# Down-projection of a gated feed-forward layer: five chunks of two tile pairs behind a plain pair, against four chunks of 2, 3, 3 and 3 pairs with no plain pair between

## The reference, cut to what matters

```python
h = _modulated_norm(x, norm_ffn_g[l], shift2, scale2)
hid = _causal_dwconv(h @ w_up[l], ffn_conv_w[l], ffn_conv_b[l])    # 3 taps, 2 x 3072 columns
act, val = jnp.split(hid, 2, axis=-1)
x = x + gate2[:, None, :] * ((jax.nn.gelu(act) * val) @ w_down[l])  # 3072 x 1024
```

## Time and profile before

| | us |
|---|---|
| median of 3 runs (lowest, highest) | 1511.46 (1511.32, 1512.23) |
| the profiled execution | 1512.01 |
| its span | 1510.3 |
| TensorE busy | 1494.3 (99%) |
| VectorE busy | 1251.8 (83%) |
| ScalarE busy | 819.4 (54%) |
| GpSimd busy | 406.9 (27%) |
| a store of a spilled block (512 KB), issue to landing, median | 2.8 to 3.0 |

### The profile page before, as it was taken

One profiled execution on the slowest core, in us unless ns is written; L12 is line 12 of the kernel. 1 busy time (PEld: TensorE's weight loads), 2 busy tenths in 40 slices (PEclk: granted clock), 3 DMA queues, 4 the chain that ended last, 5 costly groups with the idle time before them and its releaser, 6 DMA issues.

```text
span 1510.3 us, 19809 instructions
## 1 busy us (share of the span) xinstructions
PE 1494.3 (99%) x6790; PEld 1232.6 (82%) x6790; DVE 1251.8 (83%) x1584; ACT 819.4 (54%) x1237; POOL 406.9 (27%) x313
## 2 busy tenths in 40 slices
PE   7999999999999999999999999999999999999998
PEld 4888888888888888888888878888888888888887
DVE  7987888777777786698869999999999987777776
ACT  5368888734454363423436555555555553444447
POOL 0033434522222223000100233333333331333325
PEclk9999999999999999999999999999999999999999
DMA  9431233373443364572521244444444436777722
GB/s 367 174 118 57 60 91 94 121 266 115 159 139 125 109 216 146 187 225 91 172 68 34 63 167 154 155 157 152 152 152 153 154 112 233 251 251 251 251 67 112
DMA packets 212227, 231.12 MB, mean 153 GB/s; under 512 B 9920, under 2 KB 164896, under 8 KB 211360
## 3 DMA queue, kind: packets, MB, share of 16 engines
q1 hardware_dynamic: 212128, 229.86, 45.4%
HBM read 167.95 MB, written 61.87 MB: 152 GB/s over the span
## 4 chain that ended last, share of the span: by engine, by line
PE 93%; DVE 4%; DMA 1%; issue 0%; ACT 0%; SPq 0%; DVEq 0%; ACTq 0%
PE ps L900 75%; PE ps L980 6%; PE ps L1001 2%; PE ps L1285 1%; PE ps L1131 1%; PE ps L1043 1%; PE ps L1266 1%; PE ps L1188 1%; PE ps L1089 1%; DVE wop L1969 1%; DMA xtok<-in_x 1%; DVE hq L2629 1%; DVE hidw L2686 1%; DVE n L2621 0%; PE ps L1078 0%
## 5 line engine op out<-in xcount | busy, mean ns | idle before, releaser
L1361 ACT ACTIVATE wop<-raw 128x512 fp32r<-128x512 f32 (+1 forms) x541 | 307.1, 571 | 348.8 <-PE ps L900 227.8
L1969 DVE TENSOR_TENSOR wop<-raw,wop 128x512 fp32r<-128x512 f32 (+1 forms) x541 | 373.8, 695 | 103.2 <-ACT wop L1361 101.5
L733 POOL TENSOR_TENSOR raw<-raw,raw 128x512 f32<-128x512 f32 (+1 forms) x69 | 101.6, 1472 | 857.9 <-DVE wop L1969 341.6
L900 PE MATMUL ps<-hq,wop 128*128 128x512 f32 x888 | 213.7, 390 | 0.2 <-DVE hq L2629 0.2
L900 PEld LDWEIGHTS ps<-hq,wop 128*128 128x128 f32 x888 | 166.4, 188 | 36.1 <-DVE hq L2629 1.0
L900 PE MATMUL ps<-yq,wop 128*128 128x512 f32 x792 | 191.3, 390 | 0.0
L900 PE MATMUL ps<-dq,wop 128*128 128x512 f32 x840 | 190.6, 389 | 0.0
L900 PEld LDWEIGHTS ps<-dq,wop 128*128 128x128 f32 x840 | 157.7, 188 | 32.7
L900 PEld LDWEIGHTS ps<-yq,wop 128*128 128x128 f32 x792 | 148.0, 188 | 30.7
L1983 DVE TENSOR_TENSOR ps<-ps,snap_p 128x512 f32<-128x512 f32 x136 | 94.5, 695 | 43.1 <-PE ps L900 42.2
L1376 ACT ACTIVATE snap_p<-ps 128x512 f32<-128x512 f32 x136 | 81.2, 597 | 81.9 <-PE ps L900 81.7
(11 more groups left out here) (296 smaller groups left out, 2586.4 us busy)
## 6 DMA issues: line engine op xcount, KB each, us to landing
dq<-hid_keep SPq DMA_DIRECT2D x35, 1024.0 KB, 7.0
raw<-in_w_in SPq DMA_DIRECT2D x96, 256.0 KB, 4.0
raw<-in_w_up SPq DMA_DIRECT2D x96, 256.0 KB, 3.3
hid_keep<-part_b SPq DMA_DIRECT2D x40, 512.0 KB, 3.0
hid_keep<-part_t SPq DMA_DIRECT2D x20, 512.0 KB, 2.8
raw<-in_w_down SPq DMA_DIRECT2D x80, 128.0 KB, 2.3
gate_keep<-tg SPq DMA_DIRECT2D x16, 512.0 KB, 4.1
quarter_ring<-in_w_ada SPq DMA_DIRECT2D x64, 128.0 KB, 2.3
```

The source lines that it names most:

```text
L733: nc.gpsimd.tensor_tensor(s1, a21, a22, ALU.add).then_inc(s_made, 1)
L900: done = nc.tensor.matmul(bank, left[:, w, lk, :], right[:, x, rk, :], start=(first and w == 0 and x == 0), stop=(last and w == 1), skip_g ...
L1361: nc.scalar.activation(wop[n % 4][:, 0, 0:depth[n], :], raw[slot][:, 0:depth[n], :], ACT.Copy).then_inc(f_hi, 1)
L1969: V.tensor_tensor(wop[n % 4][:, 1, 0:kd, :], raw[slot_of[n][0]][:, 0:kd, :], wop[n % 4][:, 0, 0:kd, :].bitcast(F32), ALU.subtract).then_in ...
```

## The change

Eleven pairs are now spilled and go through the seven-product scheme; unit M is gone, and the four D chunks hold 2, 3, 3 and 3 pairs (16 units, D0 to D15). D0 stands right behind U23. The two-pair chunk has seven 8 KB buffers `dq_first`, all in the region that U23 reads, each filled once U23 has done the product named in `D_FIRST_FREED`. The three-pair chunks share nine 12 KB buffers, so from the third block on a block of a chunk waits until the chunk before has read a buffer in its last unit.

```diff
-        DK = 2
-        D_FREED = (1, 1, 2, 3, 3, 4, 4, 5, 5, 6, 6, 7, 7)
+        DK = 3
+        D_FIRST_AT, D_FIRST_FREED = (0, 8, 32, 40, 16, 24, 48), (1, 1, 4, 4, 6, 6, 7)
+        D_AT = [("MH", 8), ("MH", 20), ("MH", 32), ("MH", 44), ("MY", 0), ("MY", 36), ("MY", 12), ("MY", 24), ("MY", 48)]
+        D_FREED_U, D_FREED_D = (3, 3, 5, 7), (2, 4, 5, 6, 7)
...
-        NP = FT // 2 - 2
-        CHUNKS = [(c, c + DK) for c in range(0, NP, DK)]
-        SEQ += [("M", 0)] + [("D", (KT // 2) * c + i) for c in range(len(CHUNKS)) for i in range(KT // 2)] + [("L", 0)]
+        NP = FT // 2 - 1
+        CHUNKS = [(max(c, 0), c + DK) for c in range(NP % DK - DK, NP, DK)]
+        SEQ += [("D", (KT // 2) * c + i) for c in range(len(CHUNKS)) for i in range(KT // 2)] + [("L", 0)]
...
             def block_back(c, i):
+                n = 7 * (c - 1) + i
+                if c == 0:
+                    sp.wait_ge(*used_at[first_op["U", FT - 1] + D_FIRST_FREED[i] - 1])
+                elif n < len(D_FREED_U):
+                    sp.wait_ge(*used_at[first_op["U", FT - 1] + D_FREED_U[n] - 1])
...
                 elif n < len(dq):
+                    sp.wait_ge(*used_at[first_op["D", KT // 2 - 1] + D_FREED_D[n - len(D_FREED_U)] - 1])
                 else:
+                    c_before, i_before = divmod(n - len(dq), 7)
+                    sp.wait_ge(*used_at[first_op["D", KT // 2 * (c_before + 2) - 1] + i_before])
...
+                next_chunk = u // (KT // 2) + 1 if kind == "D" and u // (KT // 2) < len(CHUNKS) - 1 else None
+                ahead = 4 if next_chunk == 1 else 2
                 weights(pos, 0, 2)
+                if next_chunk is not None and u % (KT // 2) == 3:
+                    block_back(next_chunk, ahead)
...
+                if next_chunk is not None and u % (KT // 2) == 3:
+                    block_back(next_chunk, ahead + 1)
                 weights(pos, 3, 4)
+                if spilling and u == FT - 1:
+                    part_to_dram(j, "t2")
+                    block_back(0, 3)
+                    block_back(0, 4)
+                    block_back(0, 5)
+                    part_to_dram(j, "t4")
+                    part_to_dram(j, "b22")
+                    block_back(0, 6)
...
+                if next_chunk is not None and u % (KT // 2) == 3:
+                    for i in range(ahead + 2, 7):
+                        block_back(next_chunk, i)
...
-            def middle_down(m, pos):
...
+                    if (kind, u, w) == ("D", 0, 0):
+                        tap(FT - 1, 1, pos - 1)
+                    if (kind, u, w) == ("D", 0, 6):
+                        gelu(FT - 1)
+                    if (kind, u, w) == ("D", 1, 6):
+                        hid_high(FT - 1)
...
-            def middle_evict(m, pos):
...
+                    if (kind, u) == ("D", 0) and w < 4:
+                        conv_tap(FT - 1, w // 2, w % 2 + 1, pos - 1)
+                    if (kind, u, w) == ("D", 1, 3):
+                        gate_mul(FT - 1)
+                    if (kind, u, w) == ("D", 2, 3):
+                        hid_low(FT - 1)
```

More of the change, by code:

```diff
@@ L337, in plain @@
         def plain(item):
-            return item[0] in "BML" or item in (("G", 0), ("O", 3)) or item[0] == "U" and item[1] < PLAIN
+            return item[0] in "BL" or item in (("G", 0), ("O", 3)) or item[0] == "U" and item[1] < PLAIN
         def row_of(t):
@@ L702, in _ @@
                     part_to_dram(j + 1, "b11")
-                if (kind, u) == ("U", FT - 1):
-                    for i in range(3, 7):
-                        block_back(0, i)
-                if kind == "D" and u // 4 < len(CHUNKS) - 1:
-                    for i in range(2 * (u % 4), min(2 * (u % 4) + 2, 7)):
-                        block_back(u // 4 + 1, i)
+                if next_chunk is not None and u % (KT // 2) == 1:
+                    for i in range(ahead - 2):
+                        block_back(next_chunk, i)
+                if next_chunk is not None and u % (KT // 2) == 2:
+                    for i in range(ahead - 2, ahead):
+                        block_back(next_chunk, i)
+                if next_chunk is not None and u % (KT // 2) == 3:
+                    for i in range(ahead + 2, 7):
+                        block_back(next_chunk, i)
             for i in range(NB):
@@ L921, in unit @@
                 resident = YA_BLOCKS if item[0] == "A" else UP_BLOCKS if item[0] == "U" else NORM_BLOCKS
-                b11_, t1_, t2_, b22_, t3_, b21_, t4_ = resident if chunk is None else (dq[(7 * chunk + i) % len(dq)][:, :, :, :].bitcast(F32R) for i in range(7))
+                b11_, t1_, t2_, b22_, t3_, b21_, t4_ = resident if chunk is None else (dq_of(chunk, i)[:, :, :, :].bitcast(F32R) for i in range(7))
                 def t_ready(i):
@@ L1250, in _ @@
             quarter = [LB[0][:, 0, :], LB[0][:, 1, :], LB[1][:, 0, :], LB[1][:, 1, :]]
-            def middle_down(m, pos):
-                n0 = first_op["M", 0]
-                bank = BANKS[pos % 2][m % 2]
-                if m < 2:
-                    set_free(pos, m)
-                else:
-                    pe.wait_ge(down_used, m - 1)
-                for kk in range(2):
-                    n = n0 + 2 * (m // 4) + kk
-                    ready(n)
-                    pe.wait_ge(hid_lo, kk + 1)
-                    x_of = hid[hid_slot(2 * NP + kk)]
-                    for h in range(2):
-                        for w, x in PRODUCTS:
-                            done = nc.tensor.matmul(bank[:, h, :], wop[n % 4][:, w, m % 4, :], x_of[:, x, H[h]],
-                                                    start=(kk == 0 and w == 0 and x == 0), stop=(kk == 1 and w == 1))
-                done.then_inc(tile_done, 1)
             def last_down(i):
```

80 lines of the change are left out of this document (21 added, 59 removed).

## The result

| | before | changed |
|---|---|---|
| median us (lowest, highest) | 1511.46 (1511.32, 1512.23) | 1531.85 (1527.36, 1533.62) |
| ratio, 95% interval | | 1.0129 (1.0118 to 1.0141) |
| the profiled execution | 1512.01 | 1529.82 |
| its span | 1510.3 | 1527.9 |
| mean granted TensorE clock | 0.999 | 0.996 |

The changed kernel is slower, as forecast, but by 20 us and not by 7. It lies outside the range of 1511.0 to 1522.5. Its executions also spread over 6 us, those of the kernel before over 1 us.

What follows compares the result with a forecast made beforehand. TensorE, 99% busy, was taken as the bound, so time falls with fewer matmuls and rises with new waits. Terms -2.7 + 5.0 + 1.2 + 2.7 + 1.0 = +7.2 us gave 1518.7 against 1511.46; range 1511.0 to 1522.5.

Steps and rivals of the forecast that it cites:

- item 5: Ends of chunks 1 and 2: A11 lands late, join 1 ends 0.5 us late, twice: 1.0 us, from 0 to 3.
- 1, matmuls: Unit M's 96 matmuls go, D units grow from 840 to 924: 12 fewer, 2.7 us saved.
- Item 2: Loads at U23's end: A11 of D1 lands behind the backlog, D0's seventh product starts at +13.2, a 5.0 us stall.
- The lower bound of item 2: Stores free in the queue: DVE's passes decide D0's seventh product, +10.6 after U23's end, a stall of 2.4 us.
- The store's price of 1.25 us: Queue at U23's end: each half-megabyte store was taken to hold the queue for 1.25 us.
- Item 3: D1 and D2: one added DVE pass ahead of join 0 costs 0.6 us per unit, 1.2 in all.
- Item 4: End of chunk 0: A12 lands late, delaying POOL's S4, ACT's copy and snap 0; D4's third product stalls 2.7 us.
- A: Rival: the queue keeps up, only DVE's added passes are left; D0 stalls 2.4 us, total 1511.5; chance 0.12.
- B: Rival: nothing waits, so the kernel is faster, 1508.8 us, decided at D0's seventh product at +8.2; chance 0.10.
- C: Rival: queue slower with 1.5 MB blocks and stores mixed, 2.93 us per MB (358 GB/s), total 1529; chance 0.03.
- The entry of about 5 us: Expected sign: a new TensorE wait in D0 ahead of the t4 product, released by DVE's join behind a weights DMA.
- sign of being wrong: Two given: D0's seventh product starting before +10 after U23's end, or TensorE showing no wait at D4.

Runs made afterwards that it cites:

- t2_early: The changed kernel with the store of part t2 of pair 10 issued ahead of block 2 instead of behind it: 1530.78 us, ratio 1.0129.
- quarter_loads: The changed kernel with t2 stored ahead of block 2 and blocks 2 to 6 of the first chunk cut to a quarter of their bytes: 1522.80 us.
- late_stores: The changed kernel with t2 stored ahead of block 2 and the last two stores (t4, b22 of pair 10) moved behind block 6: 1531.62 us, ratio 1.0132.
- weights_first: The changed kernel with weights A22 and A12 issued ahead of the blocks in a chunk's last unit: 1529.92 us, ratio 1.0123.

## Why the prediction was wrong

The direction was right, and so was the main mechanism, loads behind a backlog once M's 21.8 us of cover are gone. Two steps failed by size: the sum of item 5, which came to 1.0 us and measured 3.9, and the price of a wait, which the forecast put at its own length, with nothing for the clock that falls behind it (5.8 us). By its items:

| item | forecast | idle in the profile | clock behind it |
|---|---|---|---|
| 1, matmuls | -2.7 | -2.7 | |
| 2, D0 | 5.0 | 2.47 + 3.09 | 3.5 |
| 3, D1 and D2 | 1.2 | 0.59 + 0.64 | |
| 4, D4 | 2.7 | 0.98 + 2.38 | 1.7 |
| 5, D8 and D12 | 1.0 | 2.20 + 1.68 | |

- **Item 2** is wrong in how it comes about and nearly right in its sum (5.6 for 5.0), which is luck. A11 landed at +14.3 instead of +11.7, because the sum began with block 2 in an idle queue, and the seventh product started at +15.8 instead of +13.2. It did not cost 2.6 more idleness there because D0 was already held for 2.47 and slowed for 1.8 before it. The chain from t2's store over ACT's buffer, two bias passes and the snap wasn't in the forecast. t2_early shows that it hides in the same delay.
- **The lower bound of item 2** (+10.6) was measured: +9.8 in quarter_loads. The store's price of 1.25 us held: in late_stores the two stores landed 1.3 us each behind what was ahead of them. Item 3 was right to a tenth, 1.23 for 1.2.
- **Item 4** named the right chain for the third product, A12, POOL's S4, copy, snap, and was short by 0.7: A12 landed at +5.7 instead of +4.7. It passed over the second product, held for 0.98 by A22 and S1, which is part of the same delay. weights_first removes both waits.
- **Item 5** is the mis-sized term: 3.9 us for 1.0. A11 came at +12.8 instead of +11.0. Of these 1.8 us, 1.0 lies again in the first load: block 2 (issued at 1360.47) took 7.5 us, not the 6.45 of a queue taken as idle. Most of the rest lies in the two weight tiles among the blocks, which landed 0.8 and 1.0 behind the block ahead, not 0.55. The blocks came 3.6 to 3.9 us apart, as taken. The bound that I gave, 3 us, was below it too.
- **Nothing on the clock.** The forecast priced a wait at its own length. Behind D0's two waits and D4's second one the clock was at half for most of 4 us: 5.8 us in all with the tenths elsewhere, and 1.3 more for the ends of eight stretches. With item 5, 2.9, and items 2 and 4, 1.2, these are 11.2 us, which makes 18.4 of 7.2. In the median there are some 2 us more than in the profiled execution. The mean granted clock was 0.996 in the two shortest executions (1527.36 and 1529.82) and 0.993 or 0.994 in the three longest, so the clock was low for longer there; which waits it followed, no profile shows.
- **The rivals.** A and B fell at D0's seventh product, which started at +15.8 and not at +10.6 or +8.2. C gave 1529, near the time, for a reason that isn't there: the stretch 1265.90 to 1270.10 moved 414 GB/s, as the earlier trace rows had it, and not 358, and the 1.5 MB blocks of D7 landed 3.6 to 3.9 us apart and not 4.4. A time that fits is no proof of its mechanism; D0's idle 5.6 us, against the 7.8 of C, speaks against it too.
- **What would show it.** The entry of about 5 us became two of 2.5 and 3.1; the one at D4 was there, and block 6 took 10.7 us to land, for 11 forecast. That last match is luck: it was issued at +3.2 and not at 0, because its place in the queue is behind the last store, whose part ACT made late, and it landed at +13.9 and not at +11.3. Neither sign of being wrong came up, so they could not have caught the error. The busy time of TensorE in the page was the first sign of the rest: fewer matmuls, more busy time.

## What to carry to other kernels

When a change takes the only work that hides a queue of loads, follow the last small load in the queue and the one buffer that is freed by a store in it, because an engine that works in order puts every join, snap and copy behind them; moving one item ahead moves the wait to the item that is now last. Price a TensorE wait of 2 us and more at its length plus up to 3 us of half clock, as these runs had it, and look at the busy time for it: it rises though the work shrinks. Start the sum of a backlog at the landing of the load that is already in the queue, not at the issue of the next one, and add every small transfer at its price when queued, before trusting a margin of half a microsecond.
